# Two edits to a fused hybrid block on one NeuronCore: the expert layer's combine joins its expert stage, with router weights loaded and cut one stage earlier, and the scan's running sums are spread by one-pass products

## The chip, the cores and the metric

The kernel runs on one core of one Trainium2 chip. The metric is the device time of one execution in microseconds (us), lower is better. Engines are called as in the profile: PE is TensorE (PEld its weight loads), DVE is VectorE, ACT is ScalarE, POOL is GpSimd, SP is SyncE; a q behind a name (SPq) is an engine's instruction queue.

## The reference, cut to what matters

Two blocks run one after the other on a sequence of 512 tokens of width 1024. The change touches only the second block, which has two layers. Each layer is a mixer, a layer norm, a mixture of experts and a layer norm:

```python
for i in range(DEPTH_2):                     # 2 layers
    mix = _ssd_mixer(...) if i % 2 == 0 else _dilated_attention_mixer(...)
    x = _layer_norm(DEEPNORM_ALPHA * x + mix, ln_g[i, 0], ln_b[i, 0])
    ffn = _hierarchical_moe(x, w_router_group[i], ..., w_gate[i], w_up[i], w_down[i])
    x = _layer_norm(DEEPNORM_ALPHA * x + ffn, ln_g[i, 1], ln_b[i, 1])
```

Inside the first mixer stands a state-space scan in 4 chunks of 128 tokens, 32 heads of 64 channels in 4 groups of 8 heads, state size 128. Its decays come from a running sum `da_cs` over each chunk:

```python
decay_in = jnp.exp(jnp.where(causal, da_cs[..., :, None] - da_cs[..., None, :], -jnp.inf))
y_diag = jnp.einsum('bcgls,bcgels,bcsgep->bclgep', cb, decay_in, xr)
```

The mixture of experts computes 4 group logits and 32 expert logits per token from `x`, picks one group and two experts in it, runs `silu(x @ w_gate) * (x @ w_up) @ w_down` of the picked experts (each weight is 1024 by 512 or 512 by 1024, three for each of 32 experts, 2 MB each), and adds the two results with their weights.

## The kernel before, in words

The program is a row of stages. A stage (`stage`, L57) is one block of code per engine; all engines meet at its end, and POOL clears the stage's semaphores. Within a stage the engines run apart and wait on semaphores. Weights of ordinary products are split by DVE into a high part rounded to fp32r and the fp32r rest (`split_weights`), and PE multiplies high by high, high by low and low by high.

**The scan** (`ssd_scan`, L2207) walks 16 units, chunk t by chunk, group g inside: unit u is (t, g), and t = 0 holds units 0 to 3. For each unit PE lays a causal wall (two 128x512 fp32r products, `wall`, L2278), adds to it the running sums of 8 heads with 8 plain fp32 products of 32x128 against a column of the identity (L2282), and computes `cb` (L2286). ACT takes 8 exponentials of 128x128 from that bank (L2338). DVE multiplies them by `cb` (L2372). PE then produces: the product with the old state (L2297, for t > 0), the new end state (L2299, for t < 3) and the inner products (16 records, L2302); later it turns a unit of three steps ago (L2311). POOL computes, in this order at step s: two scaled inputs for unit s (L2250, L2251), the decay of the state for unit s-1 (L2257, t = 1 and 2 only), then waits for the sum of unit s-1 (`summed`), then `skip` (L2262) and the gate product (L2266). DVE's `gather` (from L2374) adds it up: L2385, L2386, then, for t = 1 and 2, a wait for POOL's decay and the state's addition L2389, then L2392, which raises `summed`.

**The projection after a mixer** (`project_model`, L484) ends in `LayerNormTail` (L706): DVE mixes, ACT squares, DVE shifts (L745) and norms (L750), PE turns the tile (L591), ACT rounds it to `hT_hi` (L785) and DVE splits it to `hT_lo` (L758).

**The expert layer** (`moe`, L2428) is three stages. `moe_route` (L2452): SP loads the router's weights (L2486, L2487) and biases, stores x to `x_rows`, then begins the expert weights (L2495); DVE splits the router's weights (L277 and L279, called at L2576); PE multiplies (L2530, 32 products); a long row of small DVE operations turns logits into lists of tokens. `moe_experts` (L2662): weights stream through three slots; POOL gathers 64 token rows by an indirect DMA (L2704), PE turns and multiplies, POOL scatters the result to `y_rows` (L2659). A slot is loaded again when PE has used it (SP, L2687). `moe_combine` (L2843): SP loads the two result rows of each token as `picked` (L2867, 8 loads), then the norm's gain and bias (L719, L720), then the opening weights of the next projection; ACT scales the first result (L2882), DVE adds (L2853, L2857), and a `LayerNormTail` follows. `Opening.round_pool` (L98) is the cast of the next stage's first weights on POOL (L100).

```python
def mix(dve, t, done):                       # moe_combine
    dve.wait_ge(weighed, t + 1)              # ACT has scaled picked[:, 0, t]
    ... x = ALPHA * x + picked[:, 0, t]      # L2853
    dve.wait_ge(K.picked[2 * t + 1], 16)
    ... x = picked[:, 1, t] * weight + x     # L2857, with its row sums
```

## Time and profile before

| what | value |
|---|---|
| median of 3 runs | 3463.43 us (3453.08 to 3473.08) |
| the profiled execution | 3459.48 us, span in the trace 3457.6 us |
| PE busy | 2988.7 us (86%) |
| DVE, ACT, POOL busy | 1150.9, 860.7, 466.6 us |
| HBM read | 596.61 MB |
| mean granted PE clock | 0.913 |

A busy share of the whole program says little here: the stages have different limits. The scan takes some 130 us of it, the router of one layer some 50 us, the experts of one layer some 500 us, the combine of one layer some 40 us. So the time is read stage by stage, by what each wait ends with.

### The profile page before, as it was taken

The page shows a single profiled execution, that of the slowest core. Times are in us where ns is not written, and L with a number is a line of the kernel's source. Part 1 is how long each engine was busy: PE and PEld are TensorE (multiplying, and loading weights), DVE is VectorE, ACT ScalarE, POOL GpSimd, SP SyncE. Part 2 cuts the span into 40 slices and gives each one's busy share as a digit, 9 for nine tenths or more (in the row PEclk, how much of TensorE's full clock was granted, in tenths as well). Part 3 has the DMA queues.
Part 4 walks back from the last instruction along what each step waited for, and adds up shares of the span by engine and source line. Part 5 has one row for each costly group of instructions (what it writes and reads, how often), then busy time and mean ns, then how long its engine had stood idle before and what let it go on. Part 6 is the DMA issues. An engine that isn't in the chain of part 4 may idle for free. (4 is left out here: it accounts for less than half of the span.)

```text
span 3457.6 us, 40987 instructions
## 1 busy us (share of the span) xinstructions
PE 2988.7 (86%) x15735; PEld 2121.1 (61%) x15735; DVE 1150.9 (33%) x1827; ACT 860.7 (25%) x1739; POOL 466.6 (13%) x666
## 2 busy tenths in 40 slices
PE   7998989899989999999898688888499876888883
PEld 6777769777778878788776333333288753333331
DVE  3554754333353333346454200000353552000002
ACT  2514841332233310124541111111211431111112
POOL 0122510000000000000440011111122310111110
PEclk9998999999999999999799799899699987988897
DMA  3242023133333322221012899999443018999995
GB/s 124 86 102 74 2 74 95 41 86 86 85 97 97 97 83 94 91 79 51 1 62 87 354 382 403 402 392 401 169 129 97 21 52 346 367 401 397 390 406 198
DMA packets 250615, 605.22 MB, mean 175 GB/s; under 512 B 39829, under 2 KB 204051, under 8 KB 225788
## 3 DMA queue, kind: packets, MB, share of 16 engines
q1 hardware_dynamic: 238268, 583.05, 46.4%
q0 software_dynamic: 10880, 16.83, 1.4%
q10 hardware_dynamic: 1344, 3.67, 0.5%
q8 instruction: 80, 1.31, 0.2%
q14 instruction: 43, 0.35, 0.0%
HBM read 596.61 MB, written 24.16 MB: 180 GB/s over the span
## 5 line engine op out<-in xcount | busy, mean ns | idle before, releaser
L2745 PE MATMUL bank<-moe_raw,ex_xT 128*64 128x512 f32 x1984 | 526.9, 691 | 150.7 <-DMA moe_raw<-in_moe_w_up 147.7
L2745 PEld LDWEIGHTS bank<-moe_raw,ex_xT 128*64 128x64 f32 x1984 | 187.0, 158 | 444.4 <-issue 436.5
L2840 DVE TENSOR_TENSOR ex_h<-ex_gate,bank 64x512 f32<-64x512 f32 x64 | 44.1, 690 | 988.9 <-ACT ex_gate L2803 988.9
L248 PE MATMUL bank<-hT_hi,cut_lo 128*128 128x512 f32 x1248 | 313.1, 393 | 0.0
L248 PE MATMUL bank<-hT_hi,ahead 128*128 128x512 f32 x624 | 259.0, 415 | 28.0 <-DVEq L421 17.8
L248 PEld LDWEIGHTS bank<-hT_hi,cut_lo 128*128 128x128 f32 x1248 | 234.8, 188 | 53.0
L248 PE MATMUL bank<-hT_lo,ahead 128*128 128x512 f32 x624 | 257.0, 412 | 0.0
L248 PE MATMUL bank<-hT_hi,cut_hi 128*128 128x512 f32 x624 | 245.2, 393 | 1.1 <-DVE cut_hi L277 1.1
L248 PE MATMUL bank<-hT_lo,cut_hi 128*128 128x512 f32 x624 | 245.0, 393 | 0.0
L2762 PE MATMUL bank<-moe_raw,ex_hT 128*64 128x512 f32 x992 | 225.2, 593 | 1.3 <-ACT ex_hT L2807 1.3
L2803 ACT ACTIVATE ex_gate<-bank 64x512 f32<-64x512 f32 x64 | 37.8, 590 | 664.1 <-PE bank L2745 664.1
L2762 PEld LDWEIGHTS bank<-moe_raw,ex_hT 128*64 128x64 f32 x992 | 84.3, 137 | 128.8 <-issue 126.3
L248 PEld LDWEIGHTS bank<-hT_hi,ahead 128*128 128x128 f32 x624 | 124.1, 199 | 62.4 <-ACTq L1907 11.5
L248 PEld LDWEIGHTS bank<-hT_lo,ahead 128*128 128x128 f32 x624 | 124.1, 199 | 30.1 <-issue 0.2
L277 DVE CAST cut_hi<-raw 128x2048 fp32r<-128x2048 f32 (+1 forms) x66 | 63.8, 966 | 223.4 <-PE bank L248 136.5
L248 PEld LDWEIGHTS bank<-hT_hi,cut_hi 128*128 128x128 f32 x624 | 117.4, 188 | 27.5 <-DVE cut_hi L277 1.5
L248 PEld LDWEIGHTS bank<-hT_lo,cut_hi 128*128 128x128 f32 x624 | 117.3, 188 | 26.2 <-issue 0.2
L279 DVE TENSOR_TENSOR cut_lo<-raw,cut_hi 128x2048 fp32r<-128x2048 f32 (+1 forms) x66 | 120.2, 1821 | 2.3
L2736 PEld LDWEIGHTS bank<-ident,moe_x 64*128 64x128 f32 x528 | 63.2, 200 | 89.3 <-issue 89.3
L100 POOL CAST ahead<-raw 128x2048 fp32r<-128x2048 f32 x5 | 10.2, 2038 | 785.7 <-DMA raw<-in_ssd_w_in 385.2
L2711 POOL COPY moe_to<-moe_place 128x1 uint32 x64 | 11.6, 181 | 765.2 <-ACT moe_y L2812 765.2
L248 PE MATMUL bank<-cut_lo,hT_hi 128*128 128x256 f32 x768 | 107.3, 282 | 1.0 <-DVE cut_lo L279 0.5
(564 smaller groups left out, 5327.5 us busy)
## 6 DMA issues: line engine op xcount, KB each, us to landing
moe_raw<-in_moe_w_gate SPq DMA_DIRECT2D x62, 2048.0 KB, 14.0
moe_raw<-in_moe_w_up SPq DMA_DIRECT2D x62, 2048.0 KB, 18.5
moe_raw<-in_moe_w_down SPq DMA_DIRECT2D x62, 2048.0 KB, 9.6
raw<-in_w_in SPq DMA_DIRECT2D x26, 1024.0 KB, 5.4
raw<-in_w_ffn_in SPq DMA_DIRECT2D x44, 512.0 KB, 5.0
raw<-in_ssd_w_in SPq DMA_DIRECT2D x20, 1024.0 KB, 5.3
raw<-in_attn_w_qkv SPq DMA_DIRECT2D x18, 1024.0 KB, 5.0
raw<-in_w_in SPq DMA_DIRECT2D x24, 512.0 KB, 4.4
```

What stands on the lines that cost most here:

```text
L100: self.nc.gpsimd.tensor_copy(self.K.ahead[:, 0:self.words], self.K.raw[:, 0:self.words])
L248: last = nc.tensor.matmul(out, a(pa, k), b(pb, k), start=(late == "hi" and k == 0 and n == 0), stop=(late == "lo" and k == kt - 1 and n == ...
L277: nc.vector.tensor_copy(hi, raw).then_inc(rounded, 1)
L279: return nc.vector.tensor_tensor(lo, raw, hi.bitcast(F32), ALU.subtract)
L2711: nc.gpsimd.tensor_copy(to[:, s:s + 1], place[:, ds(b, 1)]).then_inc(directed, 1)
L2736: last = nc.tensor.transpose(TX[:, k * ER:(k + 1) * ER], x[:, s, k:D:KD], K.ident[0:ER, 0:ER])
L2745: last = nc.tensor.matmul(GU[s][rows, :], xT[:, s, k * ER:(k + 1) * ER], raw[slot][which][:, k * HID:(k + 1) * HID], start=(k == 0), stop= ...
L2762: last = nc.tensor.matmul(DB[s][rows, :], hT[:, s, k * ER:(k + 1) * ER], raw[slot][DOWN][:, k * D + half * HID:k * D + (half + 1) * HID], ...
L2803: nc.scalar.activation(gate[:, s, :], GU[s][left, :], ACT.Silu).then_inc(gate_done, 1)
L2840: nc.vector.tensor_tensor(h[:, s, :], gate[:, s, :], GU[s][right, :], ALU.mult).then_inc(h_ready, 1)
```

## The change: what it does

1. **Scan.** DVE deals the running sums out once per chunk into a high and a low fp32r part, [32, 8 heads, 128 tokens], zero where a head's row is not its own (`deal`, one 32x1024 operation and 8 of 32x128). They lie in the memory of `hT`. PE's eight fp32 products per unit become four fp32r products of 512 columns with a 0/1 group column as weights. At g = 0 PE also waits for `dealt`, ahead of the wall.
2. **Router.** `Router` loads the router's weights at the end of the projection before (behind gain and bias on SP's queue), and POOL splits them there. `moe_route` begins with its product; SP has two loads fewer ahead of the expert weights.
3. **Joined tail.** `moe_combine` is gone; its code stands behind the loops of `moe_experts`. `picked` and the square's junk lie in the weights' slot 0. Gain and bias are loaded ahead of the wait for the last scatter. DVE scales x by ALPHA once at the stage's start (128x4096), both additions are now products with the weight on DVE, and ACT scales nothing. For the attention layer the projection's `cut` is placed where `qk` lay.

```diff
@@ class Router (new)
+    def loads(self, sp):
+        sp.dma_start(self.whole[:, :, 0:EG], A.moe_w_router_group_2[layer]...).then_inc(self.loaded, 16)
+        sp.dma_start(self.whole[:, :, EG:], A.moe_w_router_expert_2[layer]...).then_inc(self.loaded, 16)
+    def split(self, pool):
+        pool.wait_ge(self.loaded, 32)
+        nc.gpsimd.tensor_copy(cut.hi[:, :, :], self.whole[:, :, :]).then_inc(self.rounded, 1)
+        pool.wait_ge(self.rounded, 1)
+        nc.gpsimd.tensor_tensor(cut.lo[:, :, :], self.whole[:, :, :], cut.hi[:, :, :].bitcast(F32), ALU.subtract)
@@ ssd_scan, spread_sums
+                    if g == 0:
+                        pe.wait_ge(dealt, t + 1)
...
-                    for e in range(SE):
-                        h = g * SE + e
-                        nc.tensor.matmul(spread_bank[:, e * P:(e + 1) * P], K.ident[0:SH, h:h + 1].broadcast_to([SH, P]), K.csT[:, toks],
-                                         start=False, stop=True, skip_group_check=True)
+                    for n, part in enumerate(dealt_sums):
+                        for b in range(2):
+                            nc.tensor.matmul(K.bank[b].rearrange("p (e l) -> p e l", e=SE // 2), of_group[:, g:g + 1].broadcast_to([SH, P]),
+                                             part[:, b * (SE // 2):(b + 1) * (SE // 2), toks], start=False, stop=(n == 1), skip_group_check=True)
@@ ssd_scan, vector
+                def deal(t):
+                    nc.vector.tensor_tensor(hi[:, :, toks], K.csT[:, toks].unsqueeze(1).broadcast_to([SH, SE, P]),
+                                            of_head[:, :].unsqueeze(2).broadcast_to([SH, SE, P]), ALU.mult).then_inc(parted, 1)
+                    dve.wait_ge(parted, t + 1)
+                    for e in range(SE):
+                        last = nc.vector.scalar_tensor_tensor(out=lo[:, e, toks], in0=K.csT[:, toks], scalar=of_head[:, e:e + 1],
+                                                              in1=hi[:, e, toks].bitcast(F32), op0=ALU.mult, op1=ALU.subtract)
+                    last.then_inc(dealt, 1)
...
                 for step in range(N + 4):
+                    if step % SG == 1 and step // SG < LAST:
+                        deal(step // SG + 1)
@@ moe_route
-                sp.dma_start(wr[:, :, 0:EG], A.moe_w_router_group_2[layer]...)
-                sp.dma_start(wr[:, :, EG:NL], A.moe_w_router_expert_2[layer]...)
-                pe.wait_ge(is_split, 1)
-                dve.wait_ge(loaded, 64)
-                split_weights(nc, dve, wr[:, :, :], cut.hi[:, :, :], cut.lo[:, :, :], rounded, 1).then_inc(is_split, 1)
@@ moe_experts, behind the loops
+                tail.loads(sp)
+                for s in range(2):
+                    sp.wait_ge(y_stored[s], n * 16 + 16)
+                for t in range(TT):
+                    for k in range(2):
+                        sp.dma_start(picked[:, k, t, :]..., rows[k * S + t * P:k * S + (t + 1) * P]).then_inc(K.picked[2 * t + k], 16)
+                if K.opening:
+                    K.opening.begin(sp)
@@ vector
+                nc.vector.tensor_scalar(K.x[:, :, :], K.x[:, :, :], ALPHA, None, ALU.mult).then_inc(x_scaled, 1)
...
+                tail.vector(dve, None)
```

**What moves on PE in the scan.** PE's rows for one unit of t = 0 before (`bank` is PSUM, `raw` holds the decays and scaled inputs, `ssd_xbc` the channels of B and C):

```order
L2278 MATMUL bank<-scan_wall,scan_one 128x512 x2
L2282 MATMUL bank<-ssd_csT,ident 128x128 x8
L2286 MATMUL bank<-ssd_xbc 128x128
L2299 MATMUL bank<-raw,ssd_xtok 128x512
L2302 MATMUL bank<-raw 128x64 x8
```

and now:

```order
L2318 MATMUL bank<-scan_wall,scan_one 128x512 x2
L2322 MATMUL bank<-hT_hi,scan_of_group 128x512 x2
L2322 MATMUL bank<-hT_lo,scan_of_group 128x512 x2
L2326 MATMUL bank<-ssd_xbc 128x128
L2339 MATMUL bank<-raw,ssd_xtok 128x512
L2342 MATMUL bank<-raw 128x64 x8
```

Nothing else of the unit has moved on PE; the eight narrow products have become four wide ones.

**What moves on DVE at the scan's start.** Before the first wall is laid DVE did two casts (L2400, L2401); now its row is this (`scan_of_head` and `scan_of_group` are the 0/1 tables):

```order
L2451 TENSOR_REDUCE scan_of_head<-ident 32x8
L2452 TENSOR_REDUCE scan_of_group_sum<-ident 32x4
L2453 CAST scan_one<-ident 128x128
L2455 CAST scan_of_group<-scan_of_group_sum 32x4
L2442 TENSOR_TENSOR hT_hi<-ssd_csT,scan_of_head 32x8x128
L2446 SCALAR_TENSOR_TENSOR hT_lo<-ssd_csT,scan_of_head,hT_hi 32x128 x8
L2458 CAST scan_wall<-scan_far 128x128
L2412 TENSOR_TENSOR raw<-raw,bank 128x1024
```

The last row is unit 0's multiplication by `cb`. The same pair L2442, L2446 stands again ahead of it for units 1, 5 and 9.

**What moves on SP at the end of an expert stage** (here of the first layer; `raw<-in_attn_w_qkv` is the next projection's opening). Before:

```order
L2867 DMA picked<-y_rows 128x2x512 x8
L719 DMA ln_g<-in_ln_g 128x1024
L720 DMA ln_b<-in_ln_b 128x1024
L112 DMA raw<-in_attn_w_qkv 128x8x256 x2
```

and now:

```order
L754 DMA ln_g<-in_ln_g 128x1024
L755 DMA ln_b<-in_ln_b 128x1024
L2771 ISA
L2776 DMA picked_12715<-y_rows 128x2x512 x8
L112 DMA raw<-in_attn_w_qkv 128x8x256 x2
```

The two small loads have moved from behind the eight picks to ahead of the wait for the scatter (the ISA row).

## Rows read from the trace of the kernel before

**Rows 1.** Windows: us, busy (x) of PE, PEld, DVE, ACT, POOL, PEclk, DMA share, GB/s

```profile
1510.00:1520.00 10.00, 10.00 (x44) 8.10 (x43) 2.19 (x2) 1.20 (x2) 0.00 (x0) 1.00 0.34 105
1660.00:1680.00 20.00, 17.67 (x66) 14.38 (x66) 3.73 (x4) 4.48 (x18) 6.38 (x7) 0.50 0.01 1
1720.00:1740.00 20.00, 20.00 (x132) 15.69 (x131) 12.53 (x18) 13.65 (x45) 15.84 (x15) 1.00 0.01 1
1948.00:1954.00 6.00, 6.00 (x25) 1.64 (x21) 0.00 (x0) 0.00 (x0) 0.00 (x0) 0.84 0.01 2
2053.00:2153.00 100.00, 80.90 (x376) 37.03 (x372) 4.14 (x6) 13.82 (x27) 15.71 (x27) 0.93 1.00 407
2710.00:2730.00 20.00, 11.62 (x58) 7.20 (x59) 9.41 (x35) 8.83 (x15) 3.69 (x5) 0.66 0.00 0
```

**Rows 2.** Timeline, scan unit of t = 1: start us, us, engine, line, operation

```profile
1718.05 1.04 POOL L2257 TENSOR_TENSOR scan_state<-scan_state,scan_last 128x512 f32<-128x512 f32 x1
1718.16 0.71 PE L2278 MATMUL bank<-scan_wall,scan_one 128*128 128x512 f32 x2
1718.80 2.05 PE L2282 MATMUL bank<-ssd_csT,ident 32*128 32x128 f32 x16
1719.20 0.68 DVE L2389 TENSOR_TENSOR scan_state<-scan_state,bank 128x512 f32<-128x512 f32 x1
1720.57 1.04 POOL L2262 TENSOR_TENSOR scan_skip<-ssd_xtok,scan_dskip 128x512 f32<-128x512 f32 x1 [1.48 <-DVE scan_mix L2392]
1720.78 0.49 PE L2286 MATMUL bank<-ssd_xbc 128*128 128x128 f32 x2
1724.80 1.04 POOL L2257 TENSOR_TENSOR scan_state<-scan_state,scan_last 128x512 f32<-128x512 f32 x1
```

**Rows 3.** Timeline, scan: walls of units 0 and 1, and of units 14 and 15

```profile
1656.29 1.22 PE L2278 MATMUL bank<-scan_wall,scan_one 128*128 128x512 f32 x2 [2.93 <-DVE scan_one L2401]
1664.27 1.22 PE L2278 MATMUL bank<-scan_wall,scan_one 128*128 128x512 f32 x2 [2.33 <-ACT raw L2338]
...
1757.83 0.70 PE L2278 MATMUL bank<-scan_wall,scan_one 128*128 128x512 f32 x2
1763.72 0.70 PE L2278 MATMUL bank<-scan_wall,scan_one 128*128 128x512 f32 x2
```

**Rows 4.** Timeline, scan: DVE's operations of 128 and of 1024 elements

```profile
1655.87 0.23 DVE L2400 CAST scan_wall<-scan_far 128x128 fp32r<-128x128 f32 x1 [3.84 <-POOL scan_far L2240]
...
1716.82 1.22 DVE L2372 TENSOR_TENSOR raw<-raw,bank 128x1024 f32<-128x1024 f32 x1 [2.49 <-ACT raw L2338]
```

**Rows 5.** Timeline, both routers: SP's first load and PE's first product

```profile
1889.64 0.38 SPq L2486 DMA_DIRECT2D rt_w<-in_moe_w_router_group  x1
1894.48 0.64 PE L2530 MATMUL bank<-hT_hi,rt_cut_hi 128*36 128x512 f32 x1 [7.42 <-DVE rt_cut_lo L279]
...
2841.91 0.38 SPq L2486 DMA_DIRECT2D rt_w<-in_moe_w_router_group  x1
2846.29 0.64 PE L2530 MATMUL bank<-hT_hi,rt_cut_hi 128*36 128x512 f32 x1 [6.96 <-DVE rt_cut_lo L279]
```

**Rows 6.** Timeline, both combines: ACT's first scaling and first square, DVE's first shift

```profile
2466.74 1.15 ACT L2882 ACTIVATE picked<-picked,moe_weight 128x1024 f32<-128x1024 f32 x1 [14.10 <-DMA picked<-y_rows]
...
2476.24 1.13 ACT L778 ACTIVATE ln_sq<-x_tok,ln_mean 128x1024 f32<-128x1024 f32 x1
...
2479.36 1.28 DVE L745 SCALAR_TENSOR_TENSOR x_tok<-x_tok,ln_mean,ln_g 128x1024 f32<-128x1024 f32 x1 [1.71 <-DMA ln_b<-in_ln_b]
...
3425.40 1.15 ACT L2882 ACTIVATE picked<-picked,moe_weight 128x1024 f32<-128x1024 f32 x1 [13.34 <-DMA picked<-y_rows]
...
3437.52 1.28 DVE L745 SCALAR_TENSOR_TENSOR x_tok<-x_tok,ln_mean,ln_g 128x1024 f32<-128x1024 f32 x1 [1.40 <-DMA ln_b<-in_ln_b]
```

**Rows 7.** Timeline, first combine: a DVE operation beside POOL's cast

```profile
2482.42 2.51 POOL L100 CAST ahead<-raw 128x2048 fp32r<-128x2048 f32 x1 [27.52 <-DMA raw<-in_attn_w_qkv]
2483.28 2.72 DVE L2857 SCALAR_TENSOR_TENSOR x_tok<-picked,moe_weight,x_tok 128x1024 f32<-128x1024 f32 x1
```

More of the change, by code:

```diff
@@ L489, in project_model @@
         raw, w_loaded = K.raw_rows, now.loaded
-        cut = Pair(mem, nc, f"cut_{nc.next_id()}", [P, SLOTS, D])
+        if cut_at is None:
+            cut = Pair(mem, nc, f"cut_{nc.next_id()}", [P, SLOTS, D])
+        else:
+            cut = Names()
+            cut.hi, cut.lo = (nc.alloc_sbuf_tensor_at(f"cut_{nc.next_id()}_{part}", [P, SLOTS, D], F32R, offset=cut_at + 4 * SLOTS * D * n)
+                              for n, part in enumerate(("hi", "lo")))
         hi_of = lambda k: K.ahead[:, 0:D] if now.ahead and k == 0 else cut.hi[:, k % SLOTS, :]
@@ L720, in loads @@
         sp.dma_start(self.b[:, :], broadcast_row(self.b_row)).then_inc(g_loaded, 16)
+        if self.router:
+            self.router.loads(sp)
     def mix(self, dve, t, done):
@@ L2224, in ssd_scan @@
         carried = [sum(1 for t, g in UNITS[:u] if 0 < t < LAST) for u in range(N + 1)]
-        with stage(nc, "loaded", "masked", "eps_set", "walled", "spread", "exped", "mixed", "scaled", "skipped", "produced", "decayed", "offset", "inner_added",
+        with stage(nc, "loaded", "masked", "eps_set", "walled", "told", "parted", "dealt", "spread", "exped", "mixed", "scaled", "skipped", "produced", "decayed", "offset", "inner_added",
                    "summed", "moved", "gated", "squared", "logged", "rooted", "normed", "turned", "rounded", "split") as (
-                block, (loaded, masked, eps_set, walled, spread, exped, mixed, scaled, skipped, produced, decayed, offset, inner_added,
+                block, (loaded, masked, eps_set, walled, told, parted, dealt, spread, exped, mixed, scaled, skipped, produced, decayed, offset, inner_added,
                         summed, moved, gated, squared, logged, rooted, normed, turned, rounded, split)):
@@ L2457, in moe_route @@
         NL = EG + NE
-        wr, br = sb("w", [P, KD, NL]), sb("b", [NL, 1])
-        cut = Pair(mem, nc, f"rt{layer}_cut", [P, KD, NL])
+        br, cut = sb("b", [NL, 1]), K.router.cut
         lgT, lg = sb("logitT", [NL, S]), sb("logit", [P, TT, NL])
@@ L2479, in moe_route @@
         wide = lambda i, n: st[:, i, :].unsqueeze(2).broadcast_to([P, TT, n])
-        with stage(nc, "loaded", "rounded", "is_split", "made", "product", "biased", "logits", "vec_step", "asked", "exped", "counted", "x_stored",
+        with stage(nc, "loaded", "made", "product", "biased", "logits", "vec_step", "asked", "exped", "counted", "x_stored",
                    "placed", "listed", "cleared") as (
-                block, (loaded, rounded, is_split, made, product_ready, biased, logits, vec_step, asked, exped, counted, x_stored, placed, listed, cleared)):
+                block, (loaded, made, product_ready, biased, logits, vec_step, asked, exped, counted, x_stored, placed, listed, cleared)):
             @block.sync
             def _(sp):
-                sp.dma_start(wr[:, :, 0:EG], A.moe_w_router_group_2[layer].rearrange("(k p) m -> p k m", p=P)).then_inc(loaded, 16)
-                sp.dma_start(wr[:, :, EG:NL], A.moe_w_router_expert_2[layer].rearrange("(k p) m -> p k m", p=P)).then_inc(loaded, 16)
                 column = lambda x: bass.AP(x.tensor, x.offset, [[1, int(np.prod(x.shape))], [1, 1]])
@@ L2660, in store_rows, with moe_experts @@
                                  in_=y[:, s, :], in_offset=None, bounds_check=4 * S - 1, oob_is_err=False).then_inc(K.y_stored[s], 16)
-def moe_experts(nc, K, A, layer, expert, pairs, idx, place, raw, x, y, to):
+def moe_experts(nc, K, A, layer, expert, pairs, idx, place, raw, x, y, to, weight, picked, tail):
     weights_d = expert_weights(A, layer)
@@ L2691, in _ @@
                 load(5, 5, 0, 4)
-                with sp.Fori(3, pairs_used(sp)) as i:
+                n = pairs_used(sp)
+                with sp.Fori(3, n) as i:
                     for s in range(2):
@@ L2695, in _ @@
                         load(b, sp.value_load(expert[0:1, ds(b, 1)], min_val=0, max_val=NE - 1), 1 - s, b - 1)
+                tail.loads(sp)
+                for s in range(2):
+                    sp.wait_ge(y_stored[s], n * 16 + 16)
+                sp.sem_inc(asked, 1)
+                rows = K.y_rows.rearrange("(h q) c -> q h c", h=2)
+                for t in range(TT):
+                    for k in range(2):
+                        sp.dma_start(picked[:, k, t, :].rearrange("p (h c) -> p h c", h=2),
+                                     rows[k * S + t * P:k * S + (t + 1) * P]).then_inc(K.picked[2 * t + k], 16)
+                if K.opening:
+                    K.opening.begin(sp)
+                if tail.dst is None:
+                    for t in range(TT):
+                        sp.wait_ge(normed, t + 1)
+                        sp.dma_start(K.out[t * P:(t + 1) * P, :], K.x[:, t, :]).then_inc(out_stored, 16)
+                    sp.wait_ge(out_stored, 16 * TT)
             @block.gpsimd
@@ L2793, in _ @@
                 down(1, n * 2 - 1, 0, n * 16)
+                tail.tensor(pe)
             @block.scalar
@@ L3196, in norm @@
     def norm(layer, n, dst, sort=False):
-        return lambda mem: LayerNormTail(mem, nc, K, A.ln_g_2[layer, n], A.ln_b_2[layer, n], dst, sort)
+        return lambda mem: LayerNormTail(mem, nc, K, A.ln_g_2[layer, n], A.ln_b_2[layer, n], dst, sort, None if n else K.router)
     for layer, mixer in enumerate((ssd, attention)):
+        K.router, K.tail_junk = Router(nc, K, A, layer), None
         mixer(nc, K, A, norm(layer, 0, K.hT))
```

113 lines of the change are left out of this document (58 added, 55 removed).

## The prediction

> **What bounds the kernel now.** I read the windows first [rows 1]. The expert loops are bound by DMA: share 1.00 at 407 GB/s while PE is busy 80.90 of 100 us. Work hidden behind the stream of weights is worth nothing there; but at the loop's start the queues stand empty (share 0.01 from 1948 to 1954), because PE has freed no slot yet. So what lies before the first expert's product, and what lies behind the last scatter, counts in full. In the scan PE is busy all the time at full clock (20.00 of 20 us), and at half clock, 0.50, in its first 25 us.
>
> Then one unit of the scan [rows 2]. PE's unit is 6.75 us, and the eight narrow products take 1.98 of it (1718.80 to 1720.78). But POOL runs a circle of its own. From its decay at 1718.05 to the next at 1724.80 it is also 6.75 us. The decay ends at 1719.09; DVE's state addition, which waits for it, starts at 1719.20; two DVE operations later POOL is released, at 1720.57; from there it works without a pause (skip, gate, two scalings) into the next decay, which carries no wait. Its floor: from skip's start to the decay's end 1724.80 + 1.04 - 1720.57 = 5.27, and from the decay's end to the next skip two additions of 0.60 and 0.69 with two semaphores, about 1.43. That makes 6.70 us against 6.75: PE and POOL bound these units together. This is the thing that the busy shares hide (POOL 15.84 of 20).
>
> **The change, part by part.** Sums are made against the profiled execution, 3459.5 us (its span 3457.6); the median of the runs is 3463.4, 3.9 above it, so I give the result against the median.
>
> *Scan, the price of a wide product.* The projection's 512-column fp32r products come 44 in 10 us at full clock [rows 1], 0.227 each; four are 0.91 instead of 1.98, so 1.07 less per unit at full clock; at half clock it would be twice that, 2.1, and I take 2.0, since loads of weights beside the products hide a little of it.
> *Its start.* DVE must deal chunk 0 before the first wall. Nearest rows [rows 4]: 1.22 for 1024 elements, 0.23 for a cast of 128, which back to back I take as 0.2. Two reductions, two casts, 1.22, 8 x 0.2, waits and the wall's own cast are 4.1 us. DVE had waited 3.84 for POOL's mask by 1655.87, and of that I count 1.6 as inside the stage, so it begins near 1654.3 and the wall can start at 1658.4 instead of 1656.29 [rows 3]: **+2.1** (bounds +1 and +4).
> *Units 0 to 3,* half or mixed clock, intervals like the 7.98 of unit 0 [rows 3]: three of 2.0 and one of 1.2, **-7.2**. Unit 4 and the products ahead of the first decay: **-2.0**.
> *Units 4 to 11,* t = 1 and 2: POOL's floor leaves 7 x 0.05; the two deals that fall here (2.8 us on DVE, which had 2.49 idle per unit [rows 4]) cost POOL's circle about 0.35 each: together **+0.3**, where PE alone would give -7.5. That is the step on which I choose.
> *Units 12 to 15,* t = 3, no decay, 5.89 apart [rows 3]: the first takes up the lead that PE has by then, 2.1; the next two gain 0.9 each, a little under PE's 1.07, since the circle of exponentials, DVE's 1.22 and its additions is then close behind PE: **-3.9**.
> Scan together: 2.1 - 7.2 - 2.0 + 0.3 - 3.9 = **-10.7**. Bounds: -18.6 if PE alone bounds all units, -4 if the slow clock lasts longer.
>
> *Router.* PE's first product stood 4.84 us behind SP's first load in layer 0 and 4.38 in layer 1 [rows 5], waiting for the load and DVE's split. Now it waits for the stage's start alone, which I put 0.35 behind SP's: -4.5 and -4.0. The loads and POOL's split go beside the projection's products, with POOL and SP idle; they cost nothing. The queues' idle 6 us shrinks by what the route gains, less 1.1 because SP begins the weights two loads earlier, so nothing of it is lost: **-8.5** (bounds -9.2 and, were the stream the bound after all, 0).
> *Scaling x by ALPHA,* 128x4096 at the stage's start: four times the 128x1024 row at most, 4.9 us; its result is wanted only behind the loops. But POOL copies its index and issues the gather in just these microseconds, and one row shows what a meeting can cost: L2857 took 2.72 beside POOL's cast, where operations of its size take 1.28 [rows 6, 7]. No row prices it here; between 0 and 2.5 us per layer I take 0.5: **+1.0**.
> The Trainium skill, GPSIMD Engine Reference, Key points, says that GpSimd shares its SBUF interfaces with VectorE and contends with instructions in a two-port mode or with two SBUF inputs. By that rule the whole scaling could stand in POOL's way, some 4 us in both layers instead of 1; the trace shows such a meeting only once [rows 7].
>
> *Joined tail.* The barrier between the scatter's landing and SP's first pick falls away: 0.3 (bounds 0 and 1). More comes from ACT: it scaled all four tiles before its first square, which therefore stood at 2476.24, 9.5 us behind the first pick at 2466.74; and DVE's first shift waited 1.71 and 1.40 more for the bias, queued behind the picks [rows 6]. Now DVE mixes as soon as the first pick is there: two tiles of 2 x 1.28, small ones 0.6, and 0.3 for picks that land later, so the shift stands 6.1 behind the pick. Layer 0: 2466.4 + 6.1 = 2472.5 instead of 2479.36, -6.9. Layer 1: 3425.1 + 6.1 = 3431.2 instead of 3437.52, -6.3. From there DVE is the bound as before, with the same operations. **-13.2** (bounds -15 and -7). What is late next is DVE's own row of shifts and norms.
>
> Sum: -10.7 - 8.5 + 1.0 - 13.2 = **-31.4**. 3463.4 - 31.4 = **3432**.
>
> **The rivals.**
> *A. PE alone bounds the scan* and POOL's circle gives way. For it: POOL's spans in a trace are rough, and the 0.05 of slack is a small difference. Against it: POOL's row from skip to decay shows no pause, and each of its waits ends at DVE's addition [rows 2]. Scan -18.6, in all -39.3: 3424.
> *B. The gather is late by what the router gained:* DVE's 4.9 us over x holds POOL's copy and descriptors back in both layers, or the stream of weights proves the bound. -31.4 + 8.5 = -22.9: 3440.5.
> *C. The scan gives nothing:* the deals stand in DVE's queue ahead of the multiplication by cb, and each pushes the whole circle by its 2.8 us, and the slow clock lasts to unit 5. -20.7: 3443.
> *D. Slower: the clock falls in the scan.* Units 4 to 11 leave PE 1.0 us without work in 6.70. From 2710 to 2730 PE was busy 11.62 of 20 us and had 0.66 of its clock [rows 1]. At half clock a unit's 5.68 us of PE work becomes 11.4, so 4.7 more for 8 units and 4.6 for three: +51, in all +20: 3483. It decides from the seventh such unit on, since 7 x 4.7 is 33. Against it: 80.90 of 100 us busy left 0.93 of the clock in the expert loop [rows 1].
> The Trainium skill, TensorE: Matmul & The Clock Gate, Part 1, says that the default state is throttled and that activity releases it. By that rule the idle 15% of these units is a danger, and the profile of the change shows the granted clock directly.
> That the change doesn't do what it says is within C and B; the picks themselves cannot come earlier than the scatter lands, and I count nothing for that.
>
> **How the numbers follow.** A change within 0.5%, 17.3 us, cannot be told from none here. My forecast 0.60, A 0.15, B 0.12, C 0.08, D 0.05. The runs of before spread over 20 us, so each case is some 6 us wide. Faster by over 0.5% means below 3446: all of the forecast and A, most of B, half of C: 0.87. Slower: 0.03, D's upper part. Same: 0.10. The range leaves out D, the far side of C and A's lower edge: 3415 to 3445.
>
> **What would show it.** In the profile after: spread products of four at 0.23 each; walls in units 5 to 11 still 6.7 apart with PE waiting for the state (A: 5.7 apart); PE clock 1.00 from unit 4 on (D: 0.5); first wall 2 us later; the router's first product within 0.5 us of SP's first load; the gather's copy as far behind the lists as before (B: 1 us or more later); the first shift 6 us behind the first pick, with no wait for the bias. The forecast is wrong if the scan's span shrinks by less than 6 or more than 15 us, or the tails by less than 10.

## The result and the profile after

| | before | after |
|---|---|---|
| median of the runs | 3465.1 us (3453.1 to 3473.1, 6 runs) | 3432.0 us (3428.7 to 3448.8, 6 runs) |
| ratio, 95% interval | | 0.9909 [0.9886, 0.9933] |
| profiled execution, its span | 3459.5, 3457.6 | 3430.3, 3428.3 |
| mean granted TensorE clock | 0.913 | 0.916 |

One execution of before (3943 us) and one of a kernel below (10736 us) stood far outside all others and are left out of the medians and ratios.

The kernel is 0.9% faster, and the forecast of 3432 was met. It was met by luck, by a sum two of whose terms were wrong: the scan gave nothing, and the tails gave nearly twice what I had counted. Distances between the same landmarks in both traces show it; they add up to the 29.3 us between the spans:

| stretch | before | after | change | forecast |
|---|---|---|---|---|
| up to SP's first load of the scan | 1654.24 | 1654.94 | +0.7 | 0 |
| scan: from that load to the projection's first cut on DVE | 130.39 | 134.93 | +4.5 | -10.7 |
| projection, to the router stage's first load | 105.01 | 104.76 | -0.3 | 0 |
| first load to PE's first router product, both layers | 4.84, 4.38 | 0.05, 0.05 | -9.1 | -8.5 |
| router's first product to POOL's copy of the index | 38.22, 38.76 | 38.65, 38.64 | +0.3 | 0 |
| that copy to the first expert product | 11.29, 12.94 | 13.16, 13.21 | +2.1 | +1.0 |
| expert loops, to the last scatter | 509.88, 515.29 | 512.84, 511.96 | -0.4 | 0 |
| last scatter to the first shift | 25.49, 24.24 | 12.70, 12.75 | -24.3 | -13.2 |
| rest of the tails | 25.10, 20.08 | 25.38, 20.87 | +1.1 | 0 |
| attention layer, to the second router's first load | 337.45 | 333.41 | -4.0 | 0 |

I take the last row for no part of the change: in the eleven traces below this stretch took 335 to 338 us, and an expert loop 506 to 518, whatever had been changed. The change itself, traced again, took 336.2 there; the mean granted clock of the stretch was 0.950 before, 0.971 after and 0.957 in that second trace.

**The scan.** These are the windows of the changed kernel (us, busy (x) of PE, PEld, DVE, ACT, POOL, PEclk, DMA share, GB/s), to be held against [rows 1]:

```profile
1655.00:1675.00 20.00, 10.44 (x25) 6.11 (x25) 11.89 (x25) 5.73 (x19) 6.08 (x8) 0.51 0.01 2
1675.00:1695.00 20.00, 19.76 (x110) 14.04 (x109) 11.99 (x15) 14.67 (x51) 15.15 (x14) 1.00 0.00 1
1695.00:1705.00 10.00, 5.91 (x31) 4.11 (x30) 9.98 (x15) 5.33 (x18) 4.60 (x5) 0.85 0.01 2
1705.00:1715.00 10.00, 10.00 (x45) 6.67 (x44) 4.49 (x7) 4.94 (x17) 7.12 (x8) 0.80 0.00 0
1725.00:1735.00 10.00, 5.71 (x30) 3.89 (x30) 9.96 (x14) 4.62 (x15) 6.37 (x5) 0.89 0.00 1
1735.00:1745.00 10.00, 8.83 (x27) 6.50 (x28) 5.18 (x9) 4.27 (x15) 5.16 (x5) 0.50 0.01 2
```

Twice DVE has no pause (9.98 and 9.96 of 10 us) while PE, never idle in this part before, is busy for less than six. What DVE does there is in its timeline (start us, us, engine, line, operation):

```profile
1693.11 1.68 DVE L2442 TENSOR_TENSOR hT_hi<-ssd_csT,scan_of_head 32x1024 fp32r<-32x1024 f32 x1
1694.82 5.43 DVE L2446 SCALAR_TENSOR_TENSOR hT_lo<-ssd_csT,scan_of_head,hT_hi 32x128 fp32r<-32x128 f32 x8
1700.19 0.67 DVE L2436 TENSOR_TENSOR hT_lo<-bank,hT_hi 128x512 fp32r<-128x512 f32 x1
1700.79 1.20 DVE L2412 TENSOR_TENSOR raw<-raw,bank 128x1024 f32<-128x1024 f32 x1
```

A deal: 7.1 us, from 1693.11 to 1700.25, where I had priced 2.8. Behind it in DVE's queue stands the multiplication by `cb` (L2412), for which PE waits:

```profile
1702.04 0.79 PE L2326 MATMUL bank<-ssd_xbc 128*128 128x128 f32 x2 [3.00 <-DVE raw L2412]
```

The four deals took 5.8, 3.4, 7.1 and 7.5 us. The eight narrow operations one by one (duration in ns, min/median/max), first over all 32 and then over four of the third deal:

```profile
L2446 DVE SCALAR_TENSOR_TENSOR hT_lo<-ssd_csT,scan_of_head,hT_hi x32: 331/333/1344, 1656.7 to 1733.0; 32x128 fp32r<-32x128 f32 x32
...
L2446 DVE SCALAR_TENSOR_TENSOR hT_lo<-ssd_csT,scan_of_head,hT_hi x4: 1119/1121/1235, 1694.8 to 1698.1; 32x128 fp32r<-32x128 f32 x4
```

POOL's timeline in these microseconds:

```profile
1695.88 1.08 POOL L2288 TENSOR_TENSOR raw<-ssd_xtok,ssd_rows 128x512 f32<-128x512 f32 x1
1696.93 1.09 POOL L2289 TENSOR_TENSOR raw<-ssd_xtok,ssd_rows 128x512 f32<-128x512 f32 x1
1697.97 1.09 POOL L2295 TENSOR_TENSOR scan_state<-scan_state,scan_last 128x512 f32<-128x512 f32 x1
```

An operation of 0.33 us takes 1.12, just longer than the 1.05 from one of POOL's operations to the next: the two engines take turns, one of DVE's for one of POOL's. Once POOL has nothing left, DVE's take 0.33 again.

Not only operations with two inputs in SBUF meet POOL. The last thing that the first wall waits for, the cast of `scan_wall`, has one input, and it falls beside a scaling of POOL:

```profile
1661.01 1.08 POOL L2288 TENSOR_TENSOR raw<-ssd_xtok,ssd_rows 128x512 f32<-128x512 f32 x1
1661.12 1.05 DVE L2458 CAST scan_wall<-scan_far 128x128 fp32r<-128x128 f32 x1
```

It took 0.23 before [rows 4]. Of all thirteen traces, the five with the old scan have it at 0.23, with nothing on POOL beside it; seven have it at 1.05 or 1.06, begun 0.1 to 0.2 us behind a scaling of POOL; in the kernel with narrow deals below it comes first, takes 0.21, and POOL's scaling takes 1.67.

PE's walls split the scan's +4.5: first wall +5.2 (7.29 behind SP's load instead of 2.05), units 0 to 3 -11.7, units 4 to 11 +15.2, units 12 to 14 -2.0, the end -2.2. The walls of units 6 and 7, 10 to 12 are at 1697.22, 1710.26, 1729.35, 1744.53 and 1754.54: 13.0 and 15.2 us where each deal holds the row up, then 10.0 at half clock. Between those of units 7 to 10 it is 5.9, 6.5 and 6.7 us: away from the deals the row closes up to POOL's circle, as forecast.

**The tails.** Before, the last scatter and the first pick of the first layer stood thus:

```profile
2453.87 1.03 POOL L2659 DMA_INDIRECT y_rows<-moe_y,moe_to  x1 [0.88 <-POOL moe_to L2711]
2462.51 0.90 SPq L2867 DMA_DIRECT2D picked<-y_rows  x2
```

Now last scatter, first pick, first mix and first shift, first and second layer:

```profile
2459.33 1.03 POOL L2715 DMA_INDIRECT y_rows<-moe_y,moe_to  x1 [0.88 <-POOL moe_to L2800]
2462.15 4.42 SPq L2776 DMA_DIRECT2D picked<-y_rows  x8
2465.70 1.28 DVE L2740 SCALAR_TENSOR_TENSOR x_tok<-picked,moe_weight,x_tok 128x1024 f32<-128x1024 f32 x1 [16.25 <-DMA picked<-y_rows]
...
2472.03 1.27 DVE L782 SCALAR_TENSOR_TENSOR x_tok<-x_tok,ln_mean,ln_g 128x1024 f32<-128x1024 f32 x1
...
3394.68 1.03 POOL L2715 DMA_INDIRECT y_rows<-moe_y,moe_to  x1 [0.88 <-POOL moe_to L2800]
...
3397.21 4.10 SPq L2776 DMA_DIRECT2D picked<-y_rows  x8
...
3407.43 1.28 DVE L782 SCALAR_TENSOR_TENSOR x_tok<-x_tok,ln_mean,ln_g 128x1024 f32<-128x1024 f32 x1
```

From the first landed pick to the shift it is 6.3 us, forecast 6.1, and no wait for the bias is left [rows 6]. But the pick itself stands 2.8 and 2.5 us behind the scatter; before it was 8.64 (2453.87 to 2462.51) and 8.69. That distance, in which I had seen 0.3 us to win, gave 5.8 and 6.2.

**Router and gather.** PE's first product has become free of SP's load [rows 5]; POOL's copy of the index has become slow:

```profile
1894.63 0.28 SPq L2547 DMA_DIRECT2D rt_b<-in_moe_b_router_group  x1
1894.68 0.61 PE L2587 MATMUL bank<-hT_hi,router_hi 128*36 128x512 f32 x1 [2.64 <-PEq L69]
...
1932.50 2.29 DVE L2929 TENSOR_SCALAR x_tok<-x_tok 128x4096 f32<-128x4096 f32 x1 [0.55 <-PEq L69]
1933.33 1.50 POOL L2790 COPY ex_col<-moe_idx 64x1 uint32<-64x1 uint32 x1 [30.34 <-issue]
1935.76 1.00 POOL L2793 DMA_INDIRECT moe_x<-x_rows,ex_col  x1 [0.92 <-POOL ex_col L2790]
```

The copy took 0.18 before and ends now, at 1934.83, with DVE's scaling of x (1934.79); in the second layer it takes 1.20 and again ends with the scaling.

### The profile page after: what moved, and what is told of

Read it like the earlier page. It is cut to its first block and busy times, and to the rows that moved or that the text cites. A ratio compares the mean times of both kernels' runs of the same rounds, so it can differ in the third digit from the quotient of the medians.

```text
span 3428.3 us, 40625 instructions
## 1 busy us (share of the span) xinstructions
PE 2976.2 (87%) x15543; PEld 2083.8 (61%) x15543; DVE 1178.4 (34%) x1864; ACT 853.5 (25%) x1731; POOL 474.6 (14%) x670
## 5 line engine op out<-in xcount | busy, mean ns | idle before, releaser
L2836 PEld LDWEIGHTS bank<-moe_raw,ex_xT 128*64 128x64 f32 x1984 | 179.5, 159 | 449.8 <-issue 442.6
L100 POOL CAST ahead<-raw 128x2048 fp32r<-128x2048 f32 x5 | 10.7, 2137 | 776.8 <-DMA raw<-in_ssd_w_in 385.1
```

The costliest lines, as they stand in the source:

```text
L100: self.nc.gpsimd.tensor_copy(self.K.ahead[:, 0:self.words], self.K.raw[:, 0:self.words])
L2836: last = nc.tensor.matmul(GU[s][rows, :], xT[:, s, k * ER:(k + 1) * ER], raw[slot][which][:, k * HID:(k + 1) * HID], start=(k == 0), stop= ...
```

## The experiments

All ratios are to the kernel before, with runs of both on the same chip. "Scan" is the distance from SP's first load to the projection's first cut on DVE; "pick" and "shift" are distances from the start of the last scatter, first and second layer.

| kernel | median us | ratio, 95% interval | scan | pick | shift |
|---|---|---|---|---|---|
| tail alone | 3445.5 | 0.9939 [0.9920, 0.9958] | 139.43 | 2.83, 2.54 | 12.87, 12.06 |
| all but the scan | 3431.8 | 0.9902 [0.9870, 0.9933] | 130.41 | 2.82, 2.54 | 12.97, 12.58 |
| scan alone | 3462.0 | 0.9985 [0.9971, 0.9999] | 134.05 | 8.64, 8.68 | 25.36, 25.16 |
| SP waits | 3465.4 | 0.9989 [0.9975, 1.0002] | 139.44 | 6.74, 6.73 | 23.85, 23.34 |
| no waits on POOL | 3463.5 | 0.9989 [0.9976, 1.0002] | 130.35 | 6.74, 6.72 | 23.66, 23.26 |
| late ALPHA | 3427.2 | 0.9882 [0.9850, 0.9913] | 134.95 | 2.83, 2.53 | 12.00, 12.51 |
| stacked parts | 3411.9 | 0.9843 [0.9813, 0.9873] | 118.79 | 2.82, 2.53 | 12.75, 11.92 |
| stacked, narrow deals | 3425.1 | 0.9879 [0.9839, 0.9920] | 131.17 | 2.82, 2.53 | 12.86, 14.02 |
| stacked, decay on DVE | 3410.9 | 0.9834 [0.9804, 0.9864] | 115.34 | 2.83, 2.52 | 12.67, 13.91 |
| the change again | 3432.4 | 0.9909 [0.9889, 0.9930] | 134.95 | 2.83, 2.53 | 12.83, 11.68 |
| ring cut | 3407.1 | 0.9830 [0.9815, 0.9844] | 112.25 | 2.83, 2.53 | 12.06, 11.71 |

The kernel with narrow deals was run twice only, the others four to ten times.

### The parts one by one

**Tail alone**: the kernel after with `ssd_scan` and `moe_route` of before and no `Router`.

> The joined tail alone: the scan and the router are those of before. My theory, from the two traces: the joining gives far more than I forecast, because the stage boundary between the last scatter and the first pick cost 5.8 us in either layer, not 0.3. Then the first pick stands 2.7 us behind the start of the last scatter (8.6 before) and the first shift 12.7 behind it (25.5 and 24.2 before), in both layers; DVE's scaling of x beside POOL's gather takes 1 to 2 us back in all; ratio 0.993 to 0.994, about 23 us less. Rival: the tails give the 13 us of the forecast and the rest of what the trace shows is chance of that execution: ratio 0.996 to 0.997.

**All but the scan**: the kernel after with `ssd_scan` of before.

> The whole change without its part in the scan (the eight narrow products and no deals). My theory: the scan's part costs 4 to 5 us, so this is faster than the whole change: ratio 0.989 to 0.990, about 36 us less than before, with the scan as long as before (130.4 us from SP's first load to the projection's first operation on DVE). Rival: the scan's part gives the 10.7 us forecast, and what the trace shows against it is chance: then this is slower than the whole change, ratio 0.993 to 0.994.

**Scan alone**: the kernel before with `ssd_scan` of after.

> The scan's part alone on the kernel before. My theory: scan 134 to 136 us from SP's first load to the projection's first operation on DVE instead of 130.4; the first wall 6 us behind where it stood; each deal 5 to 7.5 us on DVE where POOL works beside it and 3.4 where POOL is idle; time 4 to 5 us more, ratio 1.001 to 1.002. Rival: 10.7 us less, ratio 0.997.

The tail theory holds: the distances came out as written, in both layers, and 0.9939 is as expected. In the two expectations for the scan neither theory holds as I wrote it. The distances inside the scan alone came out (134.05 us; deals of 5.8, 3.4, 7.2 and 7.5 us; the first wall 5.2 later and not 6), the times didn't: the scan's part alone is not slower but 5 us faster (0.9985, an interval that reaches from -10 to 0), and leaving it out gives 0.9902 against 0.9909 for the whole change: no difference that these runs tell. The scans in the traces show one reason. The changed scan took 134.93, 134.95, 134.95 and 134.05 us in four executions; the unchanged one took 130.39, 130.41 and 130.35 in three, and 139.43 and 139.44 in two others. Windows of an unchanged scan of either kind, all but the scan first, then tail alone:

```profile
1675.00:1695.00 20.00, 20.00 (x113) 16.26 (x112) 6.07 (x8) 11.48 (x40) 10.68 (x11) 0.77 0.00 1
1695.00:1705.00 10.00, 10.00 (x68) 7.98 (x67) 6.91 (x10) 6.47 (x23) 6.14 (x6) 1.00 0.00 1
```

```profile
1675.00:1695.00 20.00, 20.00 (x79) 16.83 (x77) 4.27 (x5) 8.13 (x28) 7.94 (x8) 0.50 0.00 0
1695.00:1705.00 10.00, 10.00 (x45) 8.09 (x44) 2.99 (x5) 4.67 (x15) 4.26 (x4) 0.58 0.01 2
```

PE is busy throughout in both; its clock rises from 0.50 some 20 us later in the second (113 products against 79 in the same window), and 9 us are lost. The profile of before, on which I worked, showed the shorter kind. So the changed scan is 4.5 us longer than one kind and 4.5 shorter than the other. How often each kind comes, and what decides it, these runs don't tell; the part's worth stays open, a gain of some 5 us by the run of it alone and none by the run without it.

### What stood between the scatter and the pick

**SP waits**: the kernel before, stage boundary and all, with

```diff
@@ moe_experts, sync
+                for s in range(2):
+                    sp.wait_ge(y_stored[s], n * 16 + 16)
+                sp.sem_inc(asked, 1)
@@ moe_experts, gpsimd
                 pool.wait_ge(x_loaded[1], n * 16 + 16)
-                for s in range(2):
-                    pool.wait_ge(y_stored[s], n * 16 + 16)
-                pool.sem_inc(asked, 1)
```

> Before, with the wait for the scatter's landing moved from POOL to SP at the end of the expert stage; the stage boundary stays. It asks what the 8.6 us between the last scatter and the first pick are. Theory 1, it is POOL's own late waking from its waits behind its DMAs: with the wait on SP the pick stands about 3 us behind the scatter, in both layers, 11 us less in all, ratio 0.997. Theory 2, it is what POOL does at the boundary itself, where every engine waits for it: 8.6 stays within 0.5 us, ratio 1.000.

**No waits on POOL**: in addition POOL's wait for the last gather is moved into the combine stage, behind POOL's cast.

> Before, with all three waits that POOL had at the end of the expert stage taken from it: those for the scatters stand on SP (as in the run with SP's waits, where the pick came 6.74 us behind the last scatter instead of 8.65), that for the last gather stands behind the picks in the combine stage. Without any boundary the pick comes 2.5 to 2.8 behind. Theory 1, the remaining 3.9 us are the boundary: every engine meets POOL there, and POOL, whose queue holds the last scatter, comes late: the pick stays 6 to 7 us behind. Theory 2, they were POOL's wait for the gather: about 3 us behind.

Scatter and pick with the waits on SP, then with none on POOL:

```profile
2465.54 1.03 POOL L2659 DMA_INDIRECT y_rows<-moe_y,moe_to  x1 [0.88 <-POOL moe_to L2715]
2472.28 3.30 SPq L2868 DMA_DIRECT2D picked<-y_rows  x4
```

```profile
2452.17 1.03 POOL L2659 DMA_INDIRECT y_rows<-moe_y,moe_to  x1 [0.88 <-POOL moe_to L2716]
2458.91 5.43 SPq L2868 DMA_DIRECT2D picked<-y_rows  x8
```

Theory 1 holds of the second pair; of the first pair, neither: of the 5.8 and 6.2 us that joining gave, 1.9 were POOL's passing of its own waits for the scatters (8.65 to 6.74), and its wait for the gather was nothing (6.74 again). The other 3.9 and 4.2 us are the boundary: with no wait left on POOL they stay, and they go when the boundary goes. The ratio, 0.9989 in both kernels or 4 us, fits twice 1.9, but its interval takes in no change at all; the distances carry this reading. The scan's end, from which I took my 0.3 for a boundary, has POOL idle for microseconds; here POOL has just issued a DMA. What POOL does in those 4 us no record shows, and that stays open.

### ALPHA late

```diff
@@ moe_experts, vector
-                nc.vector.tensor_scalar(K.x[:, :, :], K.x[:, :, :], ALPHA, None, ALU.mult).then_inc(x_scaled, 1)
                 with dve.Fori(0, pairs_used(dve)) as i:
...
+                nc.vector.tensor_scalar(K.x[:, :, :], K.x[:, :, :], ALPHA, None, ALU.mult).then_inc(x_scaled, 1)
                 tail.vector(dve, None)
```

> The whole change with x's scaling by ALPHA moved from the start of the expert stage to the end of DVE's loop, where DVE is idle for 15 us before the first pick lands. My theory: POOL's copy of the index takes 0.18 us again instead of 1.2 to 1.5, the gather starts 1.1 behind the copy's start instead of 2.1 to 2.4, and the first expert product comes 1 to 2 us earlier in the first layer and up to 1 in the second, 1 to 3 us less than the whole change, which a ratio of 0.990 to 0.991 can't tell; the trace can. Rival: the first product waits for something else, and its distance from the copy stays at 13.2 us in both layers.

```profile
1931.79 0.18 POOL L2790 COPY ex_col<-moe_idx 64x1 uint32<-64x1 uint32 x1 [30.36 <-issue]
1932.90 1.00 POOL L2793 DMA_INDIRECT moe_x<-x_rows,ex_col  x1 [0.92 <-POOL ex_col L2790]
```

The copy is at 0.18 again and the gather 1.1 behind it. The first expert product comes 11.86 and 12.99 us behind the copy's start, against 13.16 and 13.21: 1.3 us in the first layer and 0.2 in the second. Over all thirteen traces this distance is 11.1 to 12.2 us in the first layer without the scaling at the stage's start and 12.6 to 13.7 with it; in the second it is 12.4 to 13.4 and 12.9 to 13.6. So the theory holds for the first layer; in the second the gather starts 1.0 earlier, and what its product gains is within the spread. The median fell by 5 us, more than this explains and within both intervals.

### The deals

**Stacked parts**: the sums' high parts on partitions 0 to 31, their low parts on 32 to 63, cut once; a deal and a spread are then

```diff
@@ spread_sums
-                    for n, part in enumerate(dealt_sums):
-                        for b in range(2):
-                            nc.tensor.matmul(..., of_group[:, g:g + 1].broadcast_to([SH, P]), part[...], start=False, stop=(n == 1), ...)
+                    for b in range(2):
+                        nc.tensor.matmul(..., of_group[:, g:g + 1].broadcast_to([2 * SH, P]), dealt_sums[...], start=False, stop=True, ...)
@@ deal
-                    nc.vector.tensor_tensor(hi[:, :, toks], K.csT..., of_head..., ALU.mult).then_inc(parted, 1)
-                    dve.wait_ge(parted, t + 1)
-                    for e in range(SE):
-                        last = nc.vector.scalar_tensor_tensor(out=lo[:, e, toks], ...)
-                    last.then_inc(dealt, 1)
+                    nc.vector.tensor_tensor(dealt_sums[:, :, toks], cs_parts[:, t:t + 1, :]..., of_head..., ALU.mult).then_inc(dealt, 1)
```

> The whole change with a cheaper deal: the high parts of the sums stand on partitions 0 to 31 and the low parts on 32 to 63 of one tile, cut once at the scan's start, so a deal is one product of 64x1024 on DVE instead of one of 32x1024 and eight of 32x128, and the spread is two products of 512 columns on PE instead of four. My theory, that the deals are what ate the scan's gain: the first wall 3.5 us behind SP's first load (2.05 before, 7.29 with the change), a deal 1.2 to 2.3 us, no unit that waits for one, scan 120 to 126 us, ratio 0.986 to 0.988. Rival: POOL's circle of 6.7 us leaves PE idle for more than a fifth of each unit, the clock falls whatever the deals do, and the scan takes 133 us or more, ratio 0.990.

**Narrow deals**: the same, but the deal's one product of 64x1024 is eight of 64x128.

> As the kernel with stacked parts, but each deal as eight products of 64x128 on DVE instead of one of 64x1024: the same elements. Theory 1, from the trace of the change (eight of 32x128 took 0.33 each alone and 1.12 beside POOL, where POOL's operations follow each other at 1.05): an operation of DVE with both inputs in SBUF waits until POOL's running operation ends, however small it is; then a deal beside POOL takes 4.5 to 6.5 us and one away from it 2.2, and the scan is 5 to 10 us longer than with one wide product. Theory 2, DVE and POOL share a port by the amount of data: 3 us at most beside POOL, and the scan within 3 us.

The third deal with one wide product, then the second and the third with eight narrow ones:

```profile
1687.14 1.68 DVE L2441 TENSOR_TENSOR hT_hi<-hT_lo,scan_of_head 64x1024 fp32r<-64x1024 f32 x1
```

```profile
1667.63 1.69 DVE L2442 TENSOR_TENSOR hT_hi<-hT_lo,scan_of_head 64x128 fp32r<-64x128 f32 x8
...
1692.57 5.79 DVE L2442 TENSOR_TENSOR hT_hi<-hT_lo,scan_of_head 64x128 fp32r<-64x128 f32 x8
```

Both deal out the same elements from the same inputs. With POOL idle the narrow deal takes 1.69 us, as much as the wide one beside POOL; with POOL busy it takes 5.79 (and 6.17 at the last), while the wide one goes from 1.21 to 1.68. The price of meeting POOL is per operation, not per element: theory 1, and theory 2's 3 us is out. The scan is 12.4 us longer with narrow deals (131.17 against 118.79), a little over the 5 to 10 expected, part of it at half clock. The Trainium skill (SBUF — State Buffer, Who interferes with whom) says that a VectorE instruction with two SBUF inputs contends with a GpSimd instruction that reads SBUF, and that the one that comes second is blocked until the other's instruction ends. By that rule every narrow operation waits out one of POOL's 1.05 us; the trace agrees with 1.12.

With the wide deal the scan gained what the change had sought: 118.79 us, 16 less than the change, below the 120 to 126 I expected, and 20 us in the median (3411.9 against 3432.0; the intervals of the ratios don't touch). Stacking also halves PE's spread, so not all of it is the deals': by the narrow deals 12.4 of the 16 us are, and the other 3.8 go with the cheaper spread and the shorter start. The first wall stood 4.15 us behind SP's load where I expected 3.5; the cast of `scan_wall` had met POOL again (1.06 us). With narrow deals the cast came first (0.21), and the wall stood at 3.78.

The rival's clock showed in part:

```profile
1715.00:1725.00 10.00, 8.08 (x39) 5.42 (x37) 6.57 (x9) 5.72 (x19) 8.60 (x8) 0.89 0.01 2
1725.00:1735.00 10.00, 10.00 (x39) 7.01 (x39) 4.30 (x6) 5.86 (x19) 6.56 (x7) 0.60 0.00 0
```

No deal stalls PE here, PE had been busy for 8 of 10 us, and the clock still fell to half for 10 us; it cost one unit of 10.0 us and one of 7.9, and the scan was short in spite of it.

### What lies behind the deals

**Decay on DVE**: stacked parts and late ALPHA; the decay of the state is taken from POOL's row and stands on DVE ahead of the state's addition.

> Stacked parts, late ALPHA, and the decay of the state moved from POOL to DVE in the units of t = 1 and 2, which takes one of five operations and a semaphore out of POOL's circle of 6.70 us. My theory, that this circle sets the distance of those units once PE is cheaper: they stand 5.3 to 5.9 us apart instead of 6.7, scan 110 to 117 us, ratio 0.982 to 0.985. Rival: DVE's decay, with both inputs in SBUF, meets POOL's operations and waits, 1.5 us or more instead of 0.68, DVE becomes the bound at 6.5 us a unit, and nothing is gained over the stacked parts.

The scan's 115.34 us and the ratio fall into my ranges, but neither mechanism came: the units stand 6.48 us apart with PE at full clock (one 7.14), and DVE's decay takes 0.68 us in seven units of eight, for POOL has run out of work by then. PE's own waits name the new bound:

```profile
1708.58 1.10 PE L2331 MATMUL bank<-scan_state,ssd_xbc 128*128 128x512 f32 x2 [0.81 <-DVE scan_state L2424]
```

PE waits until DVE, four operations behind PE's last product, has added to the state: a ring of PE and DVE in place of POOL's circle, only 0.2 us a unit shorter. The scan is 3.5 us shorter than with stacked parts alone, nearly all of it because the clock didn't fall in its middle: the two units that took 10.0 and 7.9 us take 7.1 and 6.5. **Ring cut** waits for less ahead of that product:

```diff
@@ produce
-                    if u and UNITS[u - 1][0] < LAST:
+                    if 0 < u <= SG:
                         pe.wait_ge(moved, u)
                     elif u:
-                        pe.wait_ge(inner_added, u - SG)
+                        pe.wait_ge(offset, u - SG)
...
                     if t < LAST:
+                        if u > SG:
+                            pe.wait_ge(moved, u)
...
                     pe.wait_ge(mixed, u + 1)
+                    if u > SG:
+                        pe.wait_ge(inner_added, u - SG)
```

and DVE decays the state ahead of its addition to `skip`.

> Stacked parts, late ALPHA and the decay on DVE, and PE no longer waits for DVE's addition to the state ahead of its product with the state, only ahead of the product that overwrites that bank. In the version without this the units of t = 1 and 2 stood 6.48 us apart: PE's products, then four DVE operations of 0.65, then PE again, a ring of PE and DVE in the place of POOL's. My theory: the ring falls below PE's own work of 5.3 us per unit, the units stand 5.4 to 5.9 us apart, the scan takes 107 to 111 us, ratio 0.981 to 0.983 and 5 us less than without it. Rival: the units stay at 6.4 to 6.5 us, since PE's late products wait for the multiplication by cb, and the time is 3411 as it was.

> The change itself once more, on the same chip as the version below and with the runs of before beside both. Expected: ratio 0.989 to 0.992; its scan 133 to 136 us, its picks 2.5 to 2.8 behind the scatters, the first expert product about 13.2 behind POOL's copy of the index in both layers, as in its first trace. Should its scan differ by more than 3 us from the 134.9 of that trace, the clock in the scan is what moved it.

In the ring cut, two units one after the other:

```profile
1702.04 1.04 POOL L2290 TENSOR_TENSOR raw<-ssd_xtok,ssd_rows 128x512 f32<-128x512 f32 x1
1702.25 1.38 DVE L2425 TENSOR_TENSOR scan_state<-scan_state,scan_last 128x512 f32<-128x512 f32 x1
...
1708.38 0.94 DVE L2425 TENSOR_TENSOR scan_state<-scan_state,scan_last 128x512 f32<-128x512 f32 x1
...
1708.74 1.49 POOL L2290 TENSOR_TENSOR raw<-ssd_xtok,ssd_rows 128x512 f32<-128x512 f32 x1
...
1710.28 1.13 PE L2331 MATMUL bank<-scan_state,ssd_xbc 128*128 128x512 f32 x2 [0.56 <-POOL raw L2290]
```

The units stand 6.13 to 6.27 us apart at full clock, once 6.62, between my theory and the rival. Moved forward by 0.6 us, DVE's decay now meets POOL's second scaling. Where POOL is first, the decay takes 1.30 to 1.39 us instead of 0.68 (four units of eight); where DVE is first, the scaling takes 1.49 instead of 1.04 (five times), and PE waits for it. How much of the gain the meeting takes no run tells. The scan takes 112.25 us, the whole kernel 3407.1, 25 less than the change run beside it, whose ratio and distances repeated (0.9909, scan 134.95, the first product 13.28 and 13.59 behind the copy, a little over the 13.2 expected). What cutting the ring is worth can't be told in the times (0.9830 and 0.9834). The scan is 3.1 us shorter, but that is no measure of it either: 2.6 us fall in units 0 to 3, where the clock rose 15.8 us behind SP's load instead of 23.2; units 4 to 13, where the ring is, gave 3.6; and the last two units and the end lost 3.2, with the clock at half from 1750.8 on. It is the best version here, and beats both kernels: 0.9830 [0.9815, 0.9844].

## Why the prediction was right, and where it was wrong

**What bounds the kernel**: right. The expert loops didn't change with anything, what lay ahead of them and behind them counted in full, and POOL's circle of 6.70 us is there in the changed scan (6.75 and 6.68 from decay to decay, away from the deals). Rival A's scan of PE alone didn't come; its terms add up to -18.5, not -18.6, which changes nothing.

**Price of a wide product**: nearly right, 1.11 us for four at full clock where I had 0.91, and 2.00 at half. Units 0 to 3 gained 11.7 us where I had 7.2; part of it is the clock, which was up by 1675 where it had been by about 1683 before.

**The scan's start**: the step that failed. "0.23 for a cast of 128, which back to back I take as 0.2": a cast beside an idle POOL was the row, these operations read two tiles in SBUF, and POOL had its scalings and `skip` to do; eight took 4.54 us instead of 1.6, and the wall's own cast 1.05 instead of 0.23. +5.2 instead of +2.1, outside my bound of +4.

**Units 4 to 11**: the same step again, and the larger miss. A deal of 2.8 us "cost POOL's circle about 0.35"; it took 7.1 and 7.5, and those units lost 15.2 us where the sum had +0.3 and, for unit 4, -2.0. The prediction had the means for it. It named the meeting with POOL, quoted the rule on two SBUF inputs, and had [rows 7] before it, but laid it against the scaling by ALPHA alone, which has one input, and not against nine new DVE operations set beside the busiest stretch of POOL. Rival C came nearest (each deal pushes the circle), with 2.8 for a deal where it was over 7. The units behind them, with the end, gave 4.1 for my 3.9.

**The clock in the scan**: rival D came in part. The clock fell at the deals, to 0.50 in 1735 to 1745, and one unit took 10.0 us; what idled PE most there were the waits behind DVE's deals, not the 1.0 us per unit which I had named. But with stacked parts it fell with no such stall, behind 20 us in which PE had been busy 8.0 and 8.1 of 10; with the decay on DVE it stayed up at 8.4 and 8.5 of 10. So D's own cause can act, and when it does isn't settled.

**The base**: I took the scan of before as 130.4 us. It is that or 139.4. The profiled execution was 6 us under the median of its runs, and the sums were "made against the profiled execution", so this term carries an uncertainty of 9 us that stood nowhere in my bounds.

**Router**: right, -9.1 for -8.5, and the rest of its distance was as before; nothing of it was lost to the gather, so rival B is out.

**ALPHA**: the mechanism was right and the size low by half, +2.1 for +1.0 (+1.9 and +0.3 by layer; bounds 0 to 5). Run apart it showed 1.3 and 0.2, the second within the spread. The operation took 2.29 us, not the 4.9 I had as its most. The rule that I quoted from the Trainium skill (GPSIMD Engine Reference, Key points) I had turned into 4 us; the trace shows the meeting in both layers and gives half.

**Joined tail**: mis-sized, -24.3 for -13.2. "The barrier between the scatter's landing and SP's first pick falls away: 0.3" was the term, and it measured 5.8 and 6.2. I had bounded it by the quickest boundary in the trace instead of by the distance that lay open there: scatter at 2453.87 and pick at 2462.51 were both in the trace of before. The other half, 6.1 from pick to shift, came to 6.3.

So two misses of 15 and 11 us, of opposite sign, and 4 us of the attention layer that nothing ties to the change left the sum at -29 where -31 was forecast. That the total was right is luck. The forecast named its own test, that it is wrong if the scan shrinks by less than 6; by that test it was.

## What to carry to other kernels

Before VectorE work is set beside a busy GpSimd, count its operations with two SBUF inputs, not their elements: here each cost up to one GpSimd operation, 1.1 us, so eight narrow ones cost 5.8 us and one wide one 1.7. A cast from SBUF to SBUF, with one input, waited in the same way (1.05 us instead of 0.23). Price a barrier by the distance between the last thing ahead of it and the first behind it, at that place, and not by another barrier. And when two terms rest on the clock, look at a second execution before calling one of them the base: the same code took 130 or 139 us.

## What the hardware showed that I had not expected

- Eight VectorE operations of 32x128 with two SBUF inputs: 0.33 us each alone, 1.12 beside GpSimd tensor operations that follow each other at 1.05.
- A VectorE cast of 128x128 with one SBUF input: 0.21 to 0.23 us, and 1.05 beside a GpSimd tensor operation of 128x512.
- A stage boundary right behind a DMA issued by GpSimd cost about 4 us with no wait on that engine (why stays open); at the scan's end, with GpSimd idle, one took 0.3.
- The granted clock rises from 1.2 to 2.4 GHz in the same PE-bound stretch at about 1683 in some executions and about 1704 in others.
- A one-input VectorE operation of 128x4096 holds up a GpSimd copy of one column until it ends (0.18 to 1.50 us).
